# Mixture-of-experts layer: the first expert's rows gathered early, the last tile's rows added by a one-hot product, the norm weight moved from the stored rows to the turned ones

## The reference, cut to what matters

```python
xp = xp + _mix_out(o_nsa, o_gm, out_norm_g[l], w_out[l])      # x2 in the kernel
xp = xp + _hier_moe(_rms(xp, norm2_g[l]), ...)
# _rms(x, g): x * rsqrt(mean(x*x) + EPS) * g
# _hier_moe: each token goes to 2 of 16 experts
for e in range(N_EXPERTS):
    h = jax.nn.silu(xt @ w_gate[e]) * (xt @ w_up[e])          # (n,1024) @ (1024,512), twice
    y = y + combine[:, e:e + 1] * (h @ w_down[e])             # (n,512) @ (512,1024)
```

## Time and profile before

| | us |
|---|---|
| runs, median of 3 | 718.69 (714.19, 718.69, 720.15) |
| the profiled execution's own time | 716.05 |
| its span, first to last instruction | 714.4 |
| busy: PE, PE's weight loads | 659.5, 420.1 |
| busy: DVE, ACT, POOL | 264.0, 188.8, 156.3 |
| mean granted clock of PE | 0.982 |
| moved by DMA | 185.61 MB |

### The profile page before, as it was taken

The page is one execution under the profiler, slowest core; times in us unless marked ns, Lnnn a source line. Parts: engine busy times, 40 slices in busy tenths (PEclk is TensorE's granted clock), DMA queues, the critical chain, the costliest instruction groups (busy, mean ns, idle before and its releaser), DMA issues.

```text
span 714.4 us, 14840 instructions
## 1 busy us (share of the span) xinstructions
PE 659.5 (92%) x5468; PEld 420.1 (59%) x5468; DVE 264.0 (37%) x818; ACT 188.8 (26%) x465; POOL 156.3 (22%) x237
## 2 busy tenths in 40 slices
PE   4999999999999788989999958999999999889786
PEld 1476497847646355557555435865686856456432
DVE  4148220137435666765244862112111011101216
ACT  4110212212132883576333321011111010101104
POOL 0405007230143086500032411011211111201000
PEclk9999999999999999999999987999999999999999
DMA  9995238153479086602497249999999999999973
GB/s 334 380 338 189 78 128 297 46 193 119 147 234 357 38 216 165 211 1 86 154 427 301 93 177 313 403 370 395 377 371 411 354 389 379 365 380 386 368 287 136
DMA packets 56786, 185.61 MB, mean 260 GB/s; under 512 B 9021, under 2 KB 30814, under 8 KB 50562
## 3 DMA queue, kind: packets, MB, share of 16 engines
q1 hardware_dynamic: 44914, 152.54, 56.8%
q0 software_dynamic: 11792, 32.05, 14.7%
HBM read 172.57 MB, written 13.93 MB: 261 GB/s over the span
## 4 chain that ended last, share of the span: by engine, by line
PE 74%; DMA 14%; DVE 5%; ACT 2%; issue 2%; SPq 1%; DVEq 0%; POOLq 0%; ACTq 0%
PE ps L692 68%; DMA ring<-in_w_gate_dram 6%; DMA ring<-in_w_up_dram 5%; PE ps L941 2%; PE ps L1241 1%; SPq L429 1%; DMA ring<-in_w_in_dram 1%; DMA ring<-in_cmp_pages_dram 1%; DMA h_rows<-tabs 1%; PE ps L788 1%; PE ps L968 1%; PE ps L1114 1%; ACT tabs L1682 1%; DMA ugr<-h_rows,qbd 1%; PE ps L1045 0%
## 5 line engine op out<-in xcount | busy, mean ns | idle before, releaser
L692 PE MATMUL ps<-ring,xr 128*128 128x512 f32 (+3 forms) x640 | 140.2, 416 | 9.7 <-DMA ring<-in_w_in_dram 9.7
L692 PEld LDWEIGHTS ps<-ring,xr 128*128 128x128 f32 (+1 forms) x640 | 68.9, 152 | 73.9 <-issue 60.8
L692 PE MATMUL ps<-ring,vnr 128*32 128x128 f32 (+1 forms) x1152 | 79.8, 328 | 2.6 <-DMA ring<-in_w_gate_dram 1.5
L692 PE MATMUL ps<-ring,work 128*32 128x128 f32 (+2 forms) x512 | 71.6, 369 | 0.0
L429 POOL DMA_DIRECT2D ring<-in_sel_pages_dram x96 | 51.4, 536 | 92.2 <-issue 57.0
L692 PEld LDWEIGHTS ps<-ring,vnr 128*32 128x32 f32 (+1 forms) x1152 | 54.6, 124 | 27.7 <-issue 10.6
L2878 POOL DMA_INDIRECT x_rows<-kvn,qbd x14 | 20.6, 1469 | 199.9 <-DVE kvn L2638 60.8
L2582 DVE COPY vnr<-ps 128x256 f32<-128x256 f32 (+3 forms) x16 | 8.1, 508 | 141.9 <-PE ps L1241 141.9
L692 PE MATMUL ps<-ring 128*128 128x128 f32 (+1 forms) x512 | 60.2, 279 | 0.2 <-DMA ring<-in_cmp_pages_dram 0.2
L692 PEld LDWEIGHTS ps<-ring 128*128 128x128 f32 x512 | 59.1, 191 | 0.7 <-DMA ring<-in_cmp_pages_dram 0.4
L692 PE MATMUL ps<-ring,qT 128*32 128x256 f32 (+2 forms) x320 | 52.8, 490 | 4.4 <-DMA ring<-in_w_down_dram 3.7
(11 more groups left out here) (404 smaller groups left out, 833.4 us busy)
## 6 DMA issues: line engine op xcount, KB each, us to landing
ring<-in_w_gate_dram SPq DMA_DIRECT2D x11, 2048.0 KB, 25.5
ring<-in_w_down_dram SPq DMA_DIRECT2D x10, 2048.0 KB, 30.2
ring<-in_w_up_dram SPq DMA_DIRECT2D x9, 2048.0 KB
xr<-in_w_gate_dram SPq DMA_DIRECT2D x5, 2048.0 KB, 31.8
tabs<-in_w_up_dram SPq DMA_DIRECT2D x5, 2048.0 KB, 34.2
ring<-in_cmp_pages_dram SPq DMA_DIRECT2D x64, 128.0 KB, 5.0
ring<-in_cmp_pages_dram POOLq DMA_DIRECT2D x64, 128.0 KB, 5.3
ring<-in_w_in_dram SPq DMA_DIRECT2D x3, 2048.0 KB, 9.0
```

Source lines behind the costliest of these rows:

```text
L692: return nc.tensor.matmul(out, lhsT, rhs, start=start, stop=stop)
```

## The change

The stored rows no longer carry `g2`: ACT writes `x2` times the root straight to `h2`, POOL's ten multiplies are gone, and `g2` is applied where an expert's rows are copied from PSUM to `xeT` (it lies per partition in `vec`, `g2c`). ACT does its half in four activations with a scale in place of one copy, DVE in one multiply. The 512 KB load of `g2` is gone.

POOL's two memsets of `xe` become two ACT activations with scale 0 (`rows_cleared`), after the fourth tile. POOL also stores zeros over the last tile's place in `h2_rows`.

`tokens_in_slots(3)` moves ahead of the last tile's router products and closes a sum of its own; ACT makes from its first column the numbers of expert 0's rows among the first four tiles (`first_found`). POOL gathers these 64 places before it stores the last tile. PE adds both parts of expert 0's rows in PSUM: two products with the identity (K = 64) for the gathered ones (`first_rows_gathered`, inside `positions(4)`, ahead of the last one-hot count), two with a one-hot matrix `first_here` for those of the last tile, straight from `h2` in SBUF (`first_rows_here`). ACT and DVE copy the sum back to `xe[0]`, one half each, and PE turns it.

`tokens_in_slots(4)` moves into expert 0's gate product, and with it DVE's `placed(4)` and `fixed_tokens` behind the first `rows_out`. The wait for `weights_ready` goes behind turn 1. On SP, gate 1 waits for eight router products in place of ten output products; gate 2 no longer waits for a gather, but for the last tile's router products and stores, and up 2 for the turn of expert 0.

Core of the diff:

```diff
@@ SP
-            load(g2, t["g2"].to_broadcast([P, D]), "vectors_in")
...
-            sp.wait_ge(sem("out_mm"), 2 * TILES)
+            sp.wait_ge(sem("logit_mm"), 2 * PT)
             gate_in_turn(1, 1)
-            sp.wait_ge(sem("x2_out"), 16 * (TILES + 1))
+            sp.wait_ge(sem("x2_out"), 16 * (TILES + 2))
             sp.wait_ge(sem("experts_placed"), 1)
...
-            sp.wait_ge(sem("xe_in0"), 16)
-            gate_in_turn(placed[2], 2)
             sp.wait_ge(sem("logit_mm"), 2 * TILES - 1)
             for k in range(2):
                 sp.wait_ge(sem("h2_out%d" % k), 16 * (3 - k))
+            gate_in_turn(placed[2], 2)
+            sp.wait_ge(sem("xt_mm"), 1)
             up_in_turn(placed[2], 2)
@@ PE
             def positions(r):
                 after(te, "in_slot", r)
+                if r:
+                    mm(place_counts(r), ones, run, True, False)
                 if r == PT:
-                    mm(pb[6][:, E * r:E * r + 2 * E].rearrange("p (k e) -> p k e", e=E), ones,
-                       run[:, None, :].to_broadcast([P, 2, E]), True, False)
...
+                    mm(counts, ones, run, True, False)
+                    first_rows_gathered()
                 te.wait_ge(sem("onehot_ready"), r + 1)
...
+            def first_rows_gathered():
+                te.wait_ge(sem("xe_in0"), 16)
+                for n in range(2):
+                    mm(pb[0][LIGHT_CAP * n:LIGHT_CAP * n + LIGHT_CAP, :], ident[0:LIGHT_CAP, 0:LIGHT_CAP],
+                       xe[0][0:LIGHT_CAP, W * n:W * n + W], True, False)
+
+            def first_rows_here():
+                te.wait_ge(sem("h2_ready"), TILES)
+                te.wait_ge(sem("in_slot"), TILES)
+                for n in range(2):
+                    ins = mm(pb[0][LIGHT_CAP * n:LIGHT_CAP * n + LIGHT_CAP, :], first_here, h2[0][:, W * n:W * n + W], False, True)
+                ins.then_inc(sem("slot_mm"), 1)
...
             out_product(4, 1)
+            tokens_in_slots(3)
             rows_in_columns(4, 1)
             router_parts(4)
-            tokens_in_slots(3)
             router_sum(4)
             positions(4)
-            tokens_in_slots(4)
-            te.wait_ge(sem("weights_ready"), 2)
+            first_rows_here()
...
                     for k in range(KD):
+                        if n == 0 and bank == 2 and k == 3:
+                            tokens_in_slots(4)
...
             def turn_of(n):
+                if n == 0:
+                    te.wait_ge(sem("rt_exp"), 3)
+                    te.wait_ge(sem("part_out"), TILES + 1)
+                    for k in range(KD):
+                        ins = nc.tensor.transpose(pb[4 * (k // 4)][:, P * (k % 4):P * (k % 4) + LIGHT_CAP],
+                                                  xe[0][0:LIGHT_CAP, P * k:P * k + P], ident[0:LIGHT_CAP, 0:LIGHT_CAP])
+                    ins.then_inc(sem("xt_mm"), 1)
+                    return
@@ ACT
-                act.wait_ge(sem("h2_ready"), 2 * r + 1)
-                A(h2[r % 2][0:rows, :], h2[r % 2][0:rows, :], ACT.Copy, scale=small[0:rows, 48 + i:49 + i]
+                after(act, "h2_out%d" % (r % 2), 16 * (r // 2))
+                A(h2[r % 2][0:rows, :], x2[0:rows, i, :], ACT.Copy, scale=small[0:rows, 48 + i:49 + i]
                   ).then_inc(sem("h2_ready"), 1)
+
+            def rows_cleared():
+                act.wait_ge(sem("mix_used"), TILES)
+                for n in range(2):
+                    A(xe[n].rearrange("p (c n) -> p c n", c=KD), ident[:, None, :].to_broadcast([P, KD, P]), ACT.Copy, scale=0.0).then_inc(sem("osamp_out"), 1)
...
             normed(3)
+            rows_cleared()
             square_of(4, 0)
             columns_out(4)
+            act.wait_ge(sem("slot_mm"), 1)
+            A(first_found[0:LIGHT_CAP, :], pb[1][0:LIGHT_CAP, 0:1], ACT.Copy, bias=EMPTY).then_inc(sem("osamp_out"), 1)
...
+            act.wait_ge(sem("slot_mm"), 2)
+            nc.scalar.copy(xe[0][0:LIGHT_CAP, 0:W], pb[0][0:LIGHT_CAP, :]).then_inc(sem("rt_exp"), 1)
...
-                nc.scalar.copy(xeT[par][:, 0:4, 0:cap], pb[0][:, :].rearrange("p (k n) -> p k n", k=4)[:, :, 0:cap]
-                               ).then_inc(sem("xt_ready"), 1)
+                for c in range(4):
+                    ins = A(xeT[par][:, c, 0:cap], pb[0][:, P * c:P * c + cap], ACT.Copy, scale=g2c[:, c:c + 1])
+                ins.then_inc(sem("xt_ready"), 1)
@@ DVE
-            placed(4)
+            dve.wait_ge(sem("pos_mm"), TILES)
+            V.scalar_tensor_tensor(out=first_here, in0=slot_row[:, 0:LIGHT_CAP], scalar=place_counts(PT)[:, 0:1],
+                                   in1=oh[:, PT, 0:1].to_broadcast([P, LIGHT_CAP]), op0=ALU.is_equal, op1=ALU.mult
+                                   ).then_inc(sem("in_slot"), 1)
...
             experts_weighed()
+            dve.wait_ge(sem("slot_mm"), 2)
+            V.tensor_copy(xe[0][0:LIGHT_CAP, W:2 * W], pb[0][LIGHT_CAP:2 * LIGHT_CAP, :]).then_inc(sem("part_out"), 1)
+            experts_ranked()
+            rows_out(0)
+            placed(4)
             fixed_tokens()
-            experts_ranked()
@@ POOL
-            po.wait_ge(sem("vectors_in"), 48)
             for r in range(PT):
-                times_vector(r)
                 raw_rows_stored(r)
                 rows_stored(r)
-            po.wait_ge(sem("mix_used"), TILES)
-            for k in range(2):
-                nc.gpsimd.memset(xe[k], 0.0).then_inc(sem("iota"), 1)
-            po.wait_ge(sem("iota"), 5)
-            po.dma_start(scratch_x3[TOK:TOK + CAP, :], xe[0][0:CAP, :]).then_inc(sem("x2_out"), 16)
-            times_vector(PT)
+            po.wait_ge(sem("osamp_out"), 3)
+            po.dma_start(scratch_x3[TOK:TOK + CAP, :], xe[1][0:CAP, :]).then_inc(sem("x2_out"), 16)
+            po.dma_start(scratch_h2[P * ORDER[PT]:P * ORDER[PT] + P, :], xe[1]).then_inc(sem("x2_out"), 16)
+            po.wait_ge(sem("osamp_out"), 4)
+            po.wait_ge(sem("x2_out"), 16 * (TILES + 1))
+            for k in range(2):
+                po.wait_ge(sem("h2_out%d" % k), 32)
+            po.indirect_dma_start(xe[0][0:LIGHT_CAP, :], None, scratch_h2, ...).then_inc(sem("xe_in0"), 16)
             rows_stored(PT)
             raw_rows_stored(PT)
```

More of the change, by code:

```diff
@@ L225, in hybrid_layer @@
         slot_row_i = kcs[:, P:P + CAP].bitcast(I32)
+        first_here = rt[:, 372:372 + LIGHT_CAP]
+        first_found = ints[:, 28:29]
+        EMPTY = float(2 * TOK)
         in_slot = qT[:, :, :].rearrange("p i n -> p (i n)")[:, 0:2 * TILES * P].rearrange("p (i k n) -> p i k n", i=TILES, k=2)
@@ L1156, in tokens_in_slots @@
             def tokens_in_slots(r, first=0):
-                te.wait_ge(sem("in_slot"), first + r + 1)
+                te.wait_ge(sem("in_slot"), first + r + (2 if first or r == PT else 1))
                 rows = ROWS[ORDER[r]]
+                last = r == PT and not first
                 for k in range(2):
-                    ins = mm(pb[1][0:CAP, 0:E], in_slot[0:rows, r, k, 0:CAP],
-                             slot_of[0:rows, r, k, 0, :], r == 0 and k == 0, r == PT and k == 1)
-                if r == PT:
+                    ins = mm(pb[1][0:CAP, E * last:E * last + E], in_slot[0:rows, r, k, 0:CAP], slot_of[0:rows, r, k, 0, :],
+                             k == 0 and (r == 0 or last), k == 1 and (r == PT or r == PT - 1 and not first))
@@ L1164, in tokens_in_slots @@
+                if r == PT or r == PT - 1 and not first:
                     ins.then_inc(sem("slot_mm"), 1)
@@ L2328, in _ @@
             second16 = rt[:, 456:472]
-            nowhere = work[0:CAP, 2544:2544 + E]
             def routing_prepared():
-                dve.wait_ge(sem("vectors_in"), 48)
+                dve.wait_ge(sem("vectors_in"), 32)
                 link(V.memset(work[:, 2240:2520], 0.0))
@@ L2821, in raw_rows_stored @@
                 po.dma_start(scratch_x3[i * P:i * P + rows, :], x2[0:rows, i, :]).then_inc(sem("x2_out"), 16)
-            def times_vector(r):
-                i = ORDER[r]
-                rows = ROWS[i]
-                after(po, "h2_out%d" % (r % 2), 16 * (r // 2))
-                for n in range(2):
-                    po.wait_ge(sem("x2_ready"), 2 * r + n + 1)
-                    ins = nc.gpsimd.tensor_tensor(h2[r % 2][0:rows, W * n:W * n + W], x2[0:rows, i, W * n:W * n + W],
-                                                  g2[0:rows, W * n:W * n + W], ALU.mult)
-                ins.then_inc(sem("h2_ready"), 1)
             def rows_stored(r):
@@ L2874, in added @@
                 if n == 0:
-                    po.wait_ge(sem("x2_out"), 16 * (TILES + 1))
+                    po.wait_ge(sem("x2_out"), 16 * (TILES + 2))
                 after(po, "y_added", 16 * adds_to(n))
```

76 lines of the change are left out of this document (37 added, 39 removed).

## The result

The changed kernel took 721.01 us (median of 21 runs), the kernel before, in turn with it on the same chips, 714.22 us (median of 21): a ratio of 1.0068 with a 95% interval of 1.0049 to 1.0087. The change is slower by 0.7%, where 716.3 us and a gain of 2.4 us had been predicted. The profiled execution took 720.16 us, 718.5 of them the span; the one before 716.05 and 714.4 (the median of 718.69 that the prediction started from was that of three runs only).

A forecast was written before the change was run, and what follows sets the result against it. Weight transfers bound the second half, so their start and any dry stretch count. Stream start -2.3, gather 1 in the stream +1.3, thin stretch -1.4: -2.4, from 718.69 to 716.3 us; range 711.0 to 721.5.

The forecast's parts named there:

- Front: Up to the last residual: without POOL's multiplies and memsets DVE no longer holds PE up; 1.4 us won.
- Gate 1, the zeros, the stores, ACT's copies: Earlier gate 1 and extra zeros fall where transfers idle, stores land in time, four copies are hidden: 0.
- Early gather: Expert 0's rows from the first four tiles: issued by POOL at 416.4, landed at 420.1.
- New products: Two identity and two `h2` products on PE before expert 0's first product: each pair 1.7 us fast, 3.4 slow.
- The middle column: First pair fast, rest slow: gate 2 at 429.0, 2.3 us early; expert 0's first product at 429.2, 3.7 early.
- Gather 1: Expert 1's rows: issued at 432.4, landing at 439.8 after 7.4 us; PE's wait 0 to 9, taken as 0.
- Rival 3: Gather 1 takes 16.7 us, PE idles 9.4 before turn 1, weight stream 3.2 dry: 722; chance 0.13.
- the thin place: 470 to 480 us, only 301 and 351 GB/s moved, 1.8 us lost; earlier PE mostly fills it, -1.4.
- Stream start: The weight stream begins earlier, with gate 2's earlier issue: -2.3 us.
- gather 1 inside the stream: The 0.5 MB of expert 1's gather move from idle time into the weight stream: +1.3 us.

The follow-up runs named there:

- f1_weight_moved: Kernel before with the rms weight folded into ACT's copies, without POOL's multiplies and the `g2` load, POOL's memsets kept; ratio 1.0002 to the kernel before.
- e1_list_first: Changed kernel with the whole slot table completed ahead of the ranking, so that gather 1 is issued before gate 2; ratio 0.9934 to the kernel before.
- e3_early_second: Changed kernel with expert 1's gather sent right behind the early gather, without its last-tile rows, slot table still late; ratio 0.9929 to the kernel before.

## Why the prediction was wrong

- **Front.** 1.4 us with bounds of 0 and 2.2; measured 67.38 - 65.70 = 1.68. Right. That the memset holds DVE was read from two rows, L2411 beside it at 2.41 and alone at 0.17; the runs show that 1.36 of the 1.68 are the memset's.
- **Gate 1, the zeros, the stores, ACT's copies: 0.** Right as far as the runs go: no wait of PE names the first three, and `f1_weight_moved` with ACT's copies is at 1.0002.
- **Early gather.** Forecast 1.1 us behind the beginning of the last residual (416.4 against 415.3); it came 1.0 behind (414.90 against 413.92) and was waited for 0.6 us. Right.
- **New products.** "Fast" and "slow" in the forecast are PEclk at 1.00 and at 0.50; the 20 products behind turn 1 take 2.34 us at the one and 4.30 at the other. The middle column was right in kind: the clock is 0.51 in 420 to 425. The sizes were off: the identity pair was priced at 1.7 us fast and took 1.07, the pair with `h2` at 3.4 slow and took 1.99. I had taken 0.86 for each product, from sixteen instructions for eight products; in the trace of the kernel before each of these sixteen has a weight load of its own, 0.19 us where a row shows one alone (550.45 to 556.21), which may be the difference, though no run tests it. So, counted from the last residual, the first product came 3.8 us sooner than before where 2.3 had been forecast, and gate 2 2.3 sooner where 0.9 had been.
- **Gather 1: the step that failed.** The issue was forecast well: 431.53 is 17.6 us after the last residual, 432.4 was to be 17.1. The landing was not. "The gather issued among weights at 444 took 7.4, the one at 488 took 16.7. The nearest, 7.4, gives 439.8": it took 11.24, so a wait of 5.1 us stood where 0 had been taken. In the seven kernels in which it goes out with or behind the weights it takes 10.5 to 13.4 us. The 7.4 and the 16.7 were ends of a real range, and nearness in time was no reason to prefer the one.
- **Rival 3 is what happened.** It had the mechanism, the place and the point from which it decides ("about 11 us up"), and gave 722, close to the measured median partly by luck. The 722 is 718.69 + 3.2; by the terms of the forecast's own sum, which it leaves out (-2.3 + 1.3 + 3.2), it would be 720.9, and its starting point was 4.5 us above the 714.22 of the 21 runs. Its parts were off: 9.4 us of waiting and 3.2 of dry stream, where 5.1 and 8.1 were measured. First, it names the second fall of the clock ("PE cold once more") without a price, and that fall costs 5.4 us, as much as the wait. Secondly, it gave the queue 4 us in hand at the thin place. Gate 5 came 5.3 later than before (477.28 against 471.97), the stream began 5.1 earlier and had 1.3 more to move: 5.3 + 5.1 - 1.3 = 9.1, and 8.1 of them went dry, so about 1 was in hand.
- **The sum with measured terms.** Stream start -5.1, gather 1 inside the stream +1.3, dry +8.1: +4.3. The spans differ by 718.5 - 714.4 = 4.1, the profiled executions as the runs have them too (720.16 - 716.05). 1.1 of the 5.1 are this execution's earlier load of x and not the change's; without them the sum is +5.4, beside the 4.9 us that the ratio gives.
- **What a gain ahead of the stream is worth.** The forecast let the thin place give back part of what PE gains. `e1_list_first` bears out the direction: front and seam are 1.7 + 4.6 = 6.3 us shorter than before, and its ratio is 0.0066 below 1, which is 4.7 us. About three quarters remain.
- **Chances.** 0.13 for rival 3 was too little, since nothing but the choice between 7.4 and 16.7 stood between it and the forecast. That the range of 711.0 to 721.5 held the 721.01 is luck: it was laid around 718.69, the median of three runs, from 7.7 below to 2.8 above. Around the 714.22 of 21 runs the same distances give 706.5 to 717.0, and the changed kernel lies outside. "Within 1%" (0.86) held by the ratio of 1.0068.

## What to carry to other kernels

When a change makes one transfer early by making the list of the next one late, price the next one as it will stand: among the loads that the gain itself sets going. Between a fast row and a slow row of the same transfer, ask what else was issued in the 2 us around each, and if the rows don't say, give the slow one its full chance. And a wait on PE of 5 us can cost twice that where the clock falls in it (here 5.1 and then 5.4): add the slow products behind it before calling the slack enough. A short fall can come without a wait too, as in `e3_early_second`, where it cost 1.6.

## What the hardware showed that was not expected

- In the table of the experiments gather 1 took 4.3 to 5.4 us in the four kernels where it was issued 1.3 us or more ahead of the burst of weight loads, and 10.5 to 13.4 in the seven where it was issued with it or behind it, with little between 4 and 6 MiB queued (10.53 and 11.24). In the slow case its first packet moved 4.2 to 4.8 us after the issue instead of 1.75, and from then on it shared the engines with the weights, 163 packets against 162 in the changed kernel, its own being less than a third as large (0.28 MB in 75 against 0.93 MB in 73, 437 to 440).
- A semaphore raised by POOL behind an indirect gather let SP issue 0.03 to 0.04 us after the gather's instruction began, though that instruction lasted 1.05 us: here it did not put gate 2 behind the gather.
- A POOL memset, whose row names no source, was enough to hold a DVE instruction on 128x16 elements for 2.03 us in `f1_weight_moved` and for 2.41 in the kernel before (like ones take 0.17). In both traces the DVE record begins 0.1 to 0.5 us ahead of POOL's and ends 0.03 to 0.04 behind it: 407.41 against 407.37, and 406.54 against 406.51 in the earlier trace rows. By the records' starts DVE was ahead of the memset, but POOL was then already in the store just before it (from 405.02, and from 404.12 in the trace), so the records don't say who issued first. The store alone did not hold DVE: beside the next store, from 406.81 in the trace, L2416 took its 0.17. What in the chip makes the one engine wait for the other no run shows.
- Ten small products in the gaps shortened the clock's time at its lower level from 10.2 to 6.8 us (one execution each) and moved half of what was left to expert 1's gate product, with no change of the seam.
